# One transformer block on one core: partial sums in PSUM, another load order and a GpSimd share at the start, a last row in halves at the end

## What is computed

```python
mod = silu(c) @ ada_w + ada_b
sh1, sc1, g1, sh2, sc2, g2 = split(mod, 6)
h = rms_norm(x) * (1.0 + sc1) + sh1
x = x + g1 * mlstm_mixer(h, ...)          # projections q, k, v, o, gates; 4 heads; output projection
h = rms_norm(x) * (1.0 + sc2) + sh2
x = x + g2 * swiglu(h, w_gate_up, w_down)  # d_ff = 2816
return rms_norm(x) * final_norm_w
```

## Time and profile before

| | |
|---|---|
| median of 3 runs | 1146.3 us |
| the profiled execution | 1146.06 us |
| its span, first to last instruction | 1144.2 us |
| busy: PE, DVE, ACT, POOL | 96%, 62%, 38%, 15% |
| mean granted clock of TensorE | 0.992 |

### The profile page before, as it was taken

How to read it: one execution, slowest core, us unless ns; L and a number is a source line. 1 busy time by engine, 2 the same in 40 slices (tenths; PEclk the granted TensorE clock), 3 DMA queues, 4 the chain that set the end, 5 groups by cost and what they waited for, 6 DMA issues and landing times.

```text
span 1144.2 us, 16733 instructions
## 1 busy us (share of the span) xinstructions
PE 1102.8 (96%) x6060; PEld 956.1 (84%) x6060; DVE 707.9 (62%) x1167; ACT 430.0 (38%) x761; POOL 170.6 (15%) x146
## 2 busy tenths in 40 slices
PE   5799999999999899999999999999999998999997
PEld 4598889889899899988888888888888886888886
DVE  6965725716617954666866667666766555744667
ACT  7573222212212432354433333333333326444443
POOL 2432301302324721740000000000000000000000
PEclk9899999999999999999999999999999999999999
DMA  9415514423514631202554454446444789655543
GB/s 367 153 38 174 159 47 130 134 73 111 162 46 114 217 112 53 96 38 84 173 185 142 144 196 154 146 140 205 145 149 137 271 300 348 201 187 199 189 161 147
DMA packets 86618, 178.17 MB, mean 156 GB/s; under 512 B 8056, under 2 KB 31224, under 8 KB 85520
## 3 DMA queue, kind: packets, MB, share of 16 engines
q1 hardware_dynamic: 85840, 175.07, 45.4%
q0 software_dynamic: 704, 2.13, 0.5%
HBM read 137.02 MB, written 40.16 MB: 155 GB/s over the span
## 4 chain that ended last, share of the span: by engine, by line
PE 55%; DVE 1%; DMA 0%; ACT 0%; issue 0%; SPq 0%; DVEq 0%; ACTq 0%
PE OP L1957 25%; PE O L1957 14%; PE ST L1957 5%; PE DC L1957 5%; PE AD L1957 5%; DMA dF<-w_units 0%; PE ST L1763 0%; DVE x L1605 0%; DVE x L1615 0%; PE O L1763 0%; DVE hL L1198 0%; DVE tL L1198 0%; DVE x L1622 0%; DVE dL L1558 0%; ACT junk L1001 0%
## 5 line engine op out<-in xcount | busy, mean ns | idle before, releaser
L1734 PE MATMUL OP<-wH,hH 128*128 128x256 f32 x640 | 184.6, 288 | 0.4 <-issue 0.4
L1734 PE MATMUL OP<-wH,hL 128*128 128x256 f32 x640 | 180.9, 283 | 0.0
L1734 PE MATMUL OP<-wL,hH 128*128 128x256 f32 x640 | 180.8, 283 | 0.0
L1558 DVE TENSOR_TENSOR dL<-dF,dH 128x1024 fp32r<-128x1024 f32 x77 | 92.4, 1223 | 74.8 <-ACT dH L1049 74.1
L1734 PEld LDWEIGHTS OP<-wH,hH 128*128 128x128 f32 x640 | 122.4, 191 | 3.4 <-issue 3.2
L1734 PEld LDWEIGHTS OP<-wL,hH 128*128 128x128 f32 x640 | 122.5, 191 | 0.0
L1734 PEld LDWEIGHTS OP<-wH,hL 128*128 128x128 f32 x640 | 122.4, 191 | 0.0
L1049 ACT CAST dH<-dF 128x1024 fp32r<-128x1024 f32 x77 | 79.5, 1052 | 94.8 <-DMA dF<-w_units 42.1
L1957 PE MATMUL OP<-tH,wsH 128*128 128x512 f32 x264 | 102.9, 390 | 0.0
L1957 PE MATMUL OP<-tH,wsL 128*128 128x512 f32 x264 | 102.7, 389 | 0.0
L1957 PE MATMUL OP<-tL,wsH 128*128 128x512 f32 x264 | 102.7, 389 | 0.0
(11 more groups left out here) (303 smaller groups left out, 2581.8 us busy)
## 6 DMA issues: line engine op xcount, KB each, us to landing
raw<-w_units SPq DMA_DIRECT2D x76, 512.0 KB, 4.5
dF<-act_mid SPq DMA_DIRECT2D x77, 256.0 KB, 2.7
ada<-ada_rest SPq DMA_DIRECT2D x64, 256.0 KB, 2.7
wst<-w_units SPq DMA_DIRECT2D x44, 256.0 KB, 4.7
down_mid<-wst SPq DMA_DIRECT2D x22, 512.0 KB, 3.2
dF<-down_mid SPq DMA_DIRECT2D x44, 256.0 KB, 2.9
dF<-w_units SPq DMA_DIRECT2D x33, 256.0 KB, 5.3
ada<-ada_first SPq DMA_DIRECT2D x8, 1024.0 KB, 10.0
```

The lines of the kernel that those rows point to most:

```text
L1558: nc.vector.tensor_tensor(dL[g][:], dF[g][:], dH[g][:].bitcast(F32), ALU.subtract).then_inc(d_L, 1)
L1734: ins = nc.tensor.matmul(out_ap, lhs[a], rhs[b], start=(n == 0 and i == 0), stop=(last and i == 2))
```

## The change

- SP loads rows 0 and 1 of x, then the first modulation tile and the gate weights, then the other rows.
- ScalarE does one square root on a spare element before row 0, and `mod_columns(0)` behind row 5 instead of row 2.
- The two chains of `sum1` lie in the PSUM bank AD (`SUM_BANK`); the last fused step and the closing addition write the SBUF tile `acc0`. All `mod_columns` use the bank DC, and those on TensorE wait until ScalarE has read the one before. `sum1(0)` runs behind row 1, and its columns behind the transposes of row 3.
- GpSimd scales the rows 2, 3 and 4. It splits the gate weights first and the first half of the first weights behind these rows, and takes over the second half, its high part behind k = 1 and its low part behind k = 2.
- The last output row (t = 7) is computed in column quarters 0 to 255 and 256 to 511, 33 matmuls of 256 columns each, the second in the bank O[0]; its earlier products' contribution to columns 256 to 511 is added beforehand (`end_base`).
- Of rows 4 to 7 the columns 512 to 1023 are multiplied by `fw` early on VectorE (`weighted_half`) and scaled by ScalarE (`scale_half`); VectorE finishes the other 512; each half row is a DMA of its own.

```diff
             sp.dma_start(b1[:], ada_first_b).then_inc(b1_in, 16)
-            ada_first_tile(0)
             for t in range(NT):
                 sp.dma_start(xin[:, t, :], x[t]).then_inc(x_in[t], 16)
+                if t == 1:
+                    ada_first_tile(0)
+                    sp.dma_start(wg_raw[:], w_gates).then_inc(wg_in, 16)
                 if t == 5:
                     load_unit(0, (0,))
-            sp.dma_start(wg_raw[:], w_gates).then_inc(wg_in, 16)
...
+            for t in range(4, NT):
+                sp.wait_ge(f_half, t - 3)
+                sp.dma_start(out[t][:, HALF:], x3[t][:, HALF:]).then_inc(out_done, 16)
+                sp.wait_ge(f_out, t + 1)
+                sp.dma_start(out[t][:, 0:HALF], x3[t][:, 0:HALF]).then_inc(out_done, 16)
...
+            for t in POOL_ROWS:
+                norm1(t)
+            first_high(0)
+            first_low(0)
             pool.wait_ge(m_L, 1)
             for k in range(KD):
                 for half in range(2):
...
+                        low1(k, half)
+                if k == 1:
+                    first_high(1)
+                if k == 2:
+                    first_low(1)
...
+            act.wait_ge(eps_ok, 2)
+            nc.scalar.activation(sd[:, 3 * NT - 1:3 * NT], eps[:, 0:1], ACT.Sqrt)
...
-                if k in (1, 6, 7):
-                    split_H(k // 6, k // 6, pieces=(0 if k == 6 else 1,))
+                if k in (6, 7):
+                    split_H(1, 1, pieces=(k - 6,))
...
+            def scale_half(t):
+
+                i = 2 * NT + t
+                act.wait_ge(n_rstd, i + 1)
+                act.wait_ge(weighted_ok, t - 3)
+                nc.scalar.activation(x3[t][:, HALF:], x3[t][:, HALF:], ACT.Copy,
+                                     scale=rstd[:, i:i + 1]).then_inc(f_half, 1)
...
-                even, odd = (acc0[:, k % 2, i, :] for i in range(2))
+                even, odd = (SUM_BANK[:, i * 2 * P:(i + 1) * 2 * P] for i in range(2))
...
+                        if r == KD - 1 and k >= 2:
+                            dve.wait_ge(mod1_mm, k - 1)
+                        dst = acc0[:, k % 2, :] if r == KD - 1 else acc1
+                        nc.vector.scalar_tensor_tensor(dst, ada0[:, k % 4, r, :], cact[:, r:r + 1], acc1,
                                                        ALU.mult, ALU.add).then_inc(acc0_ok, 1)
+                dve.wait_ge(acc0_ok, k * N1 + KD)
+                nc.vector.tensor_tensor(acc0[:, k % 2, :], acc0[:, k % 2, :], even, ALU.add).then_inc(acc0_ok, 1)
...
-            sum1(0)
             for t in range(NT):
+                if t == 2:
+                    sum1(0)
+                inverse(t)
                 if t >= 2:
                     evac_xT(t - 2)
-                norm1(t)
+                if t not in POOL_ROWS:
+                    norm1(t)
...
             for k in range(1, KD):
                 sum1(k)
-                if k == 3:
-                    split_L(0, 0, pieces=(1,))
...
+            def end_quarter(i):
+
+                n, t, cols = 15 + i, NT - 1, slice(i * QUARTER, (i + 1) * QUARTER)
+                dve.wait_ge(d_mm, 4 * (STEPS - NG) + 3 + i + 1)
+                dve.wait_ge(base_ok, 2)
+                bank = (DOWN_X[3], DOWN_Y[0])[i]
+                nc.vector.tensor_tensor(sB[3][:, cols], bank[:, 0:QUARTER], g2b[:, cols], ALU.mult).then_inc(d_x, 1)
+                dve.wait_ge(d_x, 2 * n + 1)
+                nc.vector.tensor_tensor(x3[t][:, cols], x3[t][:, cols], sB[3][:, cols], ALU.add).then_inc(d_x, 1)
...
             def mod_columns(k):
 
                 pe.wait_ge(acc0_ok, N1 * (k + 1))
+                if k:
+                    pe.wait_ge(mod1_ok, 2 * k)
...
+            def down_end(i):
+
+                pe.wait_ge(base_ok, 1)
+                pe.wait_ge(d_add, (8, 12)[i])
+                bank, cols = (DOWN_X[3], DOWN_Y[0])[i], slice(i * QUARTER, (i + 1) * QUARTER)
+                for g in range(NG):
+                    ins = chained(bank[:, 0:QUARTER], tuple(d[g][:, 0, 3 * P:4 * P] for d in (dH, dL)),
+                                  tuple(d[g][:, 1, cols] for d in (dH, dL)), i == 1 and g == 0, g == NG - 1)
+                ins.then_inc(d_mm, 1)
```

More of the change, by code:

```diff
@@ L35 @@
 NG = NF // 2
+QUARTER = 256
 HALF = 512
@@ L95 @@
 PLACE = {t: p for p, t in enumerate(TOKENS)}
+POOL_ROWS = (2, 3, 4)
+DVE_ROWS = tuple(t for t in range(NT) if t not in POOL_ROWS)
+HN1 = len(DVE_ROWS)
 def build(nc, x, c_col, ada_first, ada_first_b, ada_rest, ada_rest_b, w_units, w_gates, b_if, norm_w, final_w, out,
@@ L578, in _ @@
                 load_step(s)
-            for t in range(NT):
+            for t in range(4):
                 sp.wait_ge(f_out, t + 1)
                 sp.dma_start(out[t], x3[t][:]).then_inc(out_done, 16)
-            sp.wait_ge(out_done, 16 * NT)
+            for t in range(4, NT):
[3 more added lines that the diff above has]
+                sp.dma_start(out[t][:, 0:HALF], x3[t][:, 0:HALF]).then_inc(out_done, 16)
+            sp.wait_ge(out_done, 16 * (NT + 4))
         @block.gpsimd
@@ L827, in _ @@
                 root(t)
[L828 removed]
+                if t == 5:
                     act.wait_ge(b1_ok, 1)
@@ L1143, in _ @@
                 act.wait_ge(d_x, 2 * (8 + t) + 2)
-                final_square(squares, t)
+                final_square(squares, t, 2 * NT + t)
                 row_root(squares, 2 * NT + t)
                 squares += 1
-            for t in range(4, NT):
+            for t in range(4, NT - 1):
                 act.wait_ge(d_x, 2 * (8 + t) + 2)
-                final_square(squares, t, 0)
+                final_square(squares, t, 2 * NT + t, 0, HALF)
                 row_root(squares, 2 * NT + t, t)
                 squares += 1
+                if t > 4:
+                    scale_half(t - 1)
+            end = NT - 1
+            act.wait_ge(d_x, 2 * (8 + end) + 2)
+            final_square(squares, end, 3, 0, QUARTER)
+            squares += 1
+            scale_half(end - 1)
+            act.wait_ge(d_x, 2 * (8 + end) + 4)
+            final_square(squares, end, 2 * NT + end, QUARTER, HALF)
+            row_root(squares, 2 * NT + end, end)
+            squares += 1
+            scale_half(end)
         @block.vector
@@ L1714, in _ @@
                     half_ready(at_end - 3)
+                    weighted_half(at_end - 3)
+                if m == 4 and at_end == 5:
+                    end_base()
             for r in range(4):
@@ L1722, in _ @@
                     last_rows(0)
-            for r in range(1, 4):
+            for r in range(1, 3):
                 last_rows(r)
                 finish(3 + r)
+            end_quarter(0)
+            finish(NT - 2)
+            quarter_ready()
+            end_quarter(1)
             finish(NT - 1)
@@ L1769, in mod_columns @@
                 pe.wait_ge(acc0_ok, N1 * (k + 1))
+                if k:
+                    pe.wait_ge(mod1_ok, 2 * k)
                 for m in range(2):
-                    ins = nc.tensor.matmul(MOD_BANKS[k % 2][:, 2 * k + m:2 * k + m + 1],
-                                           acc0[:, k % 2, 0, m * P:(m + 1) * P], ones[:, 0:1], start=True, stop=True)
+                    ins = nc.tensor.matmul(DC[:, 2 * k + m:2 * k + m + 1], acc0[:, k % 2, m * P:(m + 1) * P],
+                                           ones[:, 0:1], start=True, stop=True)
                 ins.then_inc(mod1_mm, 1)
@@ L1788, in start @@
                         ins.then_inc(n_tr, 1)
+                    if t == 3:
+                        mod_columns(0)
                 pe.wait_ge(wg_L, 1)
@@ L2039, in _ @@
                 down_step(s)
-            for r in range(4):
+            for r in range(3):
                 down_last(r)
+            for i in range(2):
+                down_end(i)
 def kernel(x, c, ada_w, ada_b, ml_w_in, ml_b_if, ml_norm_w, ml_w_out, gdn_w_in, gdn_conv_w, gdn_a_log, gdn_dt_bias,
```

93 lines of the change are left out of this document (54 added, 39 removed).

## The result

The changed kernel takes 1137.3 us (median of 6 runs, 1137.11 to 1137.71); the kernel before, in 6 runs beside them, 1146.3 us (1142.58 to 1148.86). The ratio is 0.9928, with a 95% interval of 0.9912 to 0.9944. The forecast was 1136.2. The profiled execution took 1137.11 us, its span 1135.3, so the spans differ by 8.9 us, as the medians do.

What follows compares the result with a forecast made beforehand. TensorE was taken to be held by waits for VectorE's sums, slowed by GpSimd, and by a lowered clock. 1146.06 less 8.8 (products) and 1.3 (end) gave 1136.0, plus 0.2 for the median: 1136.2 us; range 1133.0 to 1141.5.

Steps and rivals of the forecast that it cites:

- What bounds the kernel: q/k projection: TensorE waits 7.4 us for VectorE's sums, which GpSimd slows, and loses about 2.8 us to a lower clock.
- Rival (3): Sums: the collision with GpSimd stays because the weight still comes from SBUF; only the end gains, 1145.0 us; chance 0.09.
- The price of a sum: VectorE's sum1 in PSUM: 3.6 us a sum, none blocked, no surcharge for reading or writing PSUM beyond the multiplies' lost double rate.
- rivals (2): Sums: writing PSUM costs 0.13 us an instruction, a sum 4.6; 4.7 us gained instead of 8.8, 1140.3 us; chance 0.10.
- (5): Sums: the round trip through PSUM stretches every step; at 0.35 us more each, slower at 1153.9 us; chance 0.04.
- The x rows: Up to TensorE's first product: GpSimd scaling 1.05 us a row, row stage counted at nothing, first product at 27.0.
- Rival (1): x rows: GpSimd's scaling costs as its subtraction, 2.67 us; 2.7 us later, 1138.9 us; chance 0.13.
- The other half of the step: x rows: ScalarE's 1.8 us gain is given back because VectorE's row 5 scaling is blocked until GpSimd's subtraction ends.
- The loop of products: q/k projection: products end at 62.4 against 71.16, 8.8 us less, 5.9 of it waits and the weight subtraction's queue.
- The clock: TensorE in the q/k products: no fall of the granted clock after 30 us, worth 2.9 of the 8.8 us.
- rival (4): TensorE's clock falls again after its pauses from 28.9 to 33.2; costs 2.8 us, 1139.0 us; chance 0.08.
- The end: Last stage: 66 matmuls of 256 columns cost 0.4 us, shorter work behind them saves more; together 1.3 us gained (0.5 to 1.8).

Runs made afterwards that it cites:

- experiment 1: Kernel before with only the sum1 chains in PSUM bank AD and all mod_columns in bank DC with their wait: 1136.8 us, ratio 0.9939.
- experiment 2: Changed kernel with the two sum1 chains back in SBUF, everything else as changed: 1149.4 us, ratio 1.0054 to the kernel before.
- experiment 5: Kernel before with GpSimd's low-part subtraction replaced by a one-input copy for odd k and a fill for even k: 1139.2 us, one run.
- experiment 9: The changed kernel itself, run again on another chip: 1135.7 us, ratio 0.9924 to the kernel before.
- experiment 3: Changed kernel with all eight x rows scaled by VectorE, none by GpSimd: 1135.0 us, ratio 0.9919 to the kernel before.
- experiment 6: Changed kernel with GpSimd scaling its three rows by a product with a broadcast operand: 1134.1 us, ratio 0.9903 to the kernel before.
- experiment 7: Kernel before with the last stage of the change alone, the start as before: 1144.3 us over 10 runs, ratio 0.9995.
- experiment 8: Kernel of experiment 3 with GpSimd's first weight low part subtracted in two instructions of 512 columns: 1135.1 us, ratio 0.9903 to the kernel before.

## Why the prediction was right, and where it was off

**What bounds the kernel.** Right. The gain came from the two places named, the waits for sums and the clock. Experiment 1 has the one without the rest of the change, experiment 2 the rest without the one, and experiment 5 names the cause: GpSimd's reading of SBUF beside a VectorE step with two SBUF inputs. Rival (3), that the collision stays, is out.

**The price of a sum.** 3.77 us for 3.6. The steps and the addition have the lengths forecast; the next sum's first multiply starts 0.53 us behind the addition (46.94 to 47.47), where 0.36 was counted. The forecast overlooked a wait that the change adds: each sum now waits for the addition before it, since both use one bank, and with the chains in SBUF (experiment 2) the distance is 0.54 as well. Writing PSUM costs nothing else, so rivals (2) and (5) are out. The rule of the Trainium skill that spoke against it, "VectorE: DVE Perf Modes", § The TRN2 errata, with more fixed cycles for PSUM than for SBUF, is not borne out: five steps with a PSUM input and output take 2.05 us, and with SBUF in experiment 2 they take 2.06. What the multiplies lose is the double rate alone (a pair 0.87 for 0.61).

**The x rows.** Here a step failed: GpSimd's scaling was taken as its cast, 1.05 us, for having one tensor input. It costs 2.83, a little above the other end of the range, 2.67. Rival (1) is what happened: the first product came 3.2 us late, with 2.7 counted for it; in experiment 9 it came 2.0 late. Experiments 3 and 6 show it from both sides, at 26.57 without GpSimd's share and 26.60 with a price of 1.88. Against experiment 9, 0.55 of it is a later load (ScalarE came to row 2 at 11.57, not at 10.99, with 10.6 to 11.0 counted) and 0.7 the slower transposes. The other half of the step held: ScalarE's 1.8 us is given back at a scaling of VectorE's that GpSimd blocks (experiment 3 against 1), only that in the full change it is rows 5 and 6, held up for 0.8 and 0.7 us, and not row 5 alone.

**The loop of products.** From first product to the 256-column product 34.6 us for 35.4 forecast. k = 1 starts 6.3 us behind k = 0, with 6.7 counted; k = 3 starts 0.25 late (44.97 for 44.72), with 0.6 counted. The 0.8 is a gift of the late first product, since VectorE's sums had run ahead of it: in experiment 9, where it came 1.25 earlier, two waits for sums are left (0.67 and 1.20 us), k = 1 starts 7.0 behind k = 0, and the loop takes 35.3. The new wait of `mod_columns` for ScalarE shows in no row. By experiments 1 and 3 the move of the second weight half to GpSimd gives 0.6, with a late k = 3 of that size already taken off. The products' end moved by 6.4 us (7.0 in experiment 9), with 8.8 counted. The prediction had set 6 as the least for being right, so this was close.

**The clock.** Right for the loop: behind the first product the granted clock stays at 1.00 to the end of the products, and every later product of 512 columns takes 0.39 to 0.50 us, so rival (4) is out. How near the loop was to a fall the runs don't tell. Not forecast was that TensorE stays at the lower level for longer among the x rows: its transposes are slow until 25.4 us in experiment 9 and until the first product in the first profile of the change, where the kernel before was back at the upper level from about 24 us.

**The end.** 66 matmuls of 256 columns cost 0.43 more (0.4 forecast). Behind the last one 1.41 us went, with 1.7 counted: the final step took 0.75 for 0.68, and the two halves' sends follow each other on SP by 0.4. In total 1.0 for 1.3, in the range of 0.5 to 1.8; experiment 7 has 0.9.

**What was not forecast.** By the terms as measured (6.4 at the products' end, 1.0 in the last stage) the change should have given 7.4 us of span; it gave 8.9. The 1.5 in between come in three parts, found by comparing the starts of the same matmuls in the two profiles. The lead of 6.4 us grows to 7.0 in the first heads, where TensorE waits less for VectorE's `PT`, first before, then after:

```profile
115.76 0.70 PE L1914 MATMUL O<-C,qs 128*128 128x257 f32 x2 [1.36 <-DVE PT L1329]
```

```profile
108.74 0.70 PE L2011 MATMUL O<-C,qs 128*128 128x257 f32 x2 [0.72 <-DVE PT L1379]
```

This wait is 0.95 in experiment 9 and 1.36 again in experiments 1, 3 and 7, so both profiles of the change have it shorter; why is not shown. At 385 to 390 us the lead grows to 8.4, at two waits of the profile before that the one after has not. The timeline of TensorE before:

```profile
387.21 1.02 PE L1837 MATMUL AD<-acc,ones 128*1 128x512 f32 x2 [0.98 <-DVE acc L1395]
...
388.98 1.09 PE L1856 MATMUL ST<-ident,hg 128*128 128x128 f32 x8 [0.74 <-POOL hg L650]
```

Both stand in no other profile of this study, not in that of experiment 7 either, whose first stage and heads are those of the kernel before, nor in experiment 2's, whose heads begin latest. So they belong to that one execution rather than to the kernel. Up to the down products' last chain the lead falls back to 7.9.

That does not close the term: in the medians the change is 8.8 us under the kernel before on the chip of experiment 9 too, where the steps give 7.0 and 1.0. From the products' end to the span's end the eight profiles with the new first stage (with its variations) and the new last one take 1068.7 to 1072.9 us, and the kernel before 1073.0; a spread of 4 us in which the rest can't be assigned. It stays open. It nearly made up for what GpSimd's scaling cost, and that is luck: the time came within 1.1 us of the forecast although the products' end came 2.4 us later than forecast. Measured by its steps, 1137.3 is rival (1) at 1138.9, less this 1.5.

## What to carry to other kernels

When VectorE runs a chain of accumulations beside GpSimd, put the accumulator in PSUM: with its second SBUF input gone, the chain keeps its speed (five steps 2.05 us, not 4.13), and here that is most of a gain of 0.7%. Before work goes to an idle engine on the way to the first product, measure that operation there and not its neighbour; GpSimd's "idle" 13.75 to 22.24 was three times 2.83 us in series where VectorE needed 0.75 each. And where a block between two engines is moved, look where it lands next: it held up rows 5 and 6 in the change, row 4 in experiment 3 and row 5 in experiment 8.

## What the runs showed of the hardware

- GpSimd, 1024 fp32 columns: cast 1.03, broadcast product 1.88, subtraction of two tensors 2.68, scaling by a per-partition value 2.83, by a constant 2.76 us. The product with a broadcast second operand is cheaper than the scaling with one tensor input.
- VectorE's steps with two SBUF inputs lose time beside GpSimd's two-input subtractions (2.06 to 4.13) and beside its one-input copies (2.46 to 2.81), not beside its fills (2.46). Steps with one SBUF input and PSUM for the rest lose nothing (five in 2.05 beside the subtractions).
- The loss is mutual: GpSimd's pair took 3.54 us beside VectorE's weight subtraction in experiment 1, and 2.53 to 2.67 beside the sums in PSUM.
- VectorE's scaling from SBUF to SBUF waits for a GpSimd subtraction that started just before it: 2.88 us, begun 0.02 behind it, for 0.74 alone.
- Two profiles of one kernel differ by 1.2 us at the first product (28.94 and 30.19): 0.55 by a later load, the rest with TensorE's last transposes at 1.10 us and at 1.97 us for eight. In the slower one the clock column shows 1.00 all the same.
